# Three buffers instead of two for loaded weight pieces, with the low part written over the piece it is computed from

## What is computed

```python
def _layer(x, mem, cos, sin, w_in, ...):            # first block, twice
    h = x @ w_in
    ...
    y_mla, y_sb, y_fox, y_mem = ...
    merged = merged + merge_g[:, :, n] * (yb @ w_branch[n])
    out = merged @ w_out
    return _layer_norm(DEEPNORM_ALPHA * x + out, ln_g, ln_b)

def second_block(x, norm_g, w_in, w_out, ...):      # second block, twice
    h = _rmsnorm(x, norm_g[l])
    z = jnp.einsum('bsd,de->bse', h, w_in[l])
    ...
    q_a = _axial_rope(q_a, row, col)                # A; then B (window), D (differential), C (neighbourhood)
    k_a = _axial_rope(k_a, row, col)
    ...
    x = x + jnp.einsum('bsm,md->bsd', mix, w_out[l])
```

## Time and profile before

| | |
|---|---|
| median of 3 runs | 1443.2 us (1442.56 to 1445.12) |
| the profiled execution | 1443.2 us, its span 1441.4 us |
| TensorE matmul | busy 1371.9 us, 95% of the span |
| VectorE | busy 864.6 us, 60% |
| ScalarE | busy 732.6 us, 51% |
| GpSimd | busy 382.0 us, 27% |
| granted TensorE clock, mean | 0.988 of full speed |
| DMA | 94 GB/s on average over the span |

### The profile page before, as it was taken

One profiled execution on the slowest core, in us unless ns is written; L12 is line 12 of the kernel. 1 busy time (PEld: TensorE's weight loads), 2 busy tenths in 40 slices (PEclk: granted clock), 3 DMA queues, 4 the chain that ended last, 5 costly groups with the idle time before them and its releaser, 6 DMA issues.

```text
span 1441.4 us, 20050 instructions
## 1 busy us (share of the span) xinstructions
PE 1371.9 (95%) x7466; PEld 1064.1 (74%) x7466; DVE 864.6 (60%) x1513; ACT 732.6 (51%) x1561; POOL 382.0 (27%) x273
## 2 busy tenths in 40 slices
PE   7999999999989999999998899999899999999897
PEld 7877788778787777887776777776766877675665
DVE  4656536557662564455577675568656665578555
ACT  4555447655344554556554464446444554546443
POOL 2233131346131322213554111421012111421111
PEclk9999999999999999999999999999999999999999
DMA  7413551125353221112265532511323443511311
GB/s 236 118 31 92 115 142 48 52 72 224 102 161 65 55 88 59 59 48 66 77 229 167 130 74 59 125 59 52 103 67 90 111 93 70 113 59 23 118 51 59
DMA packets 185894, 135.65 MB, mean 94 GB/s; under 512 B 91334, under 2 KB 166726, under 8 KB 185798
## 3 DMA queue, kind: packets, MB, share of 16 engines
q1 hardware_dynamic: 182022, 120.22, 30.9%
q10 hardware_dynamic: 3776, 14.16, 2.5%
HBM read 122.03 MB, written 12.32 MB: 93 GB/s over the span
## 4 chain that ended last, share of the span: by engine, by line
PE 72%; DVE 14%; ACT 7%; issue 2%; POOL 2%; DMA 1%; SPq 1%; DVEq 0%; ACTq 0%; POOLq 0%
PE pb L1650 18%; PE pb L1652 17%; PE pb L1651 17%; PE pb L1741 5%; PE pb L1690 5%; PE pb L1717 5%; ACT prob L1797 3%; ACT tmp L1797 2%; DVE prob L2420 2%; DVE wl L2167 2%; SPq L2698 1%; PE pb L1772 1%; DMA tbias<-zscr 1%; PE pb L1726 1%; POOL wl L2564 1%
## 5 line engine op out<-in xcount | busy, mean ns | idle before, releaser
L2564 POOL TENSOR_TENSOR wl<-wr,wh 128x512 fp32r<-128x512 f32 x178 | 253.5, 1424 | 706.3 <-ACT wh L1817 702.1
L1650 PE MATMUL pb<-xh,wl 128*128 128x512 f32 (+1 forms) x880 | 350.2, 398 | 11.9 <-DVE wl L2167 6.4
L1652 PE MATMUL pb<-xh,wh 128*128 128x512 f32 (+1 forms) x880 | 324.8, 369 | 0.0
L1651 PE MATMUL pb<-xl,wh 128*128 128x512 f32 (+1 forms) x880 | 324.3, 369 | 0.0
L2167 DVE TENSOR_TENSOR wl<-wr,wh 128x512 fp32r<-128x512 f32 x208 | 167.2, 806 | 175.3 <-ACT wh L1817 175.1
L1817 ACT CAST wh<-wr 128x512 fp32r<-128x512 f32 (+1 forms) x386 | 220.1, 606 | 36.2 <-PE pb L1652 22.1
L1650 PEld LDWEIGHTS pb<-xh,wl 128*128 128x128 f32 x880 | 167.3, 190 | 65.6 <-issue 29.5
L1652 PEld LDWEIGHTS pb<-xh,wh 128*128 128x128 f32 x880 | 167.1, 190 | 29.1
L1651 PEld LDWEIGHTS pb<-xl,wh 128*128 128x128 f32 x880 | 167.9, 191 | 24.6 <-issue 4.3
L1797 ACT ACTIVATE tmp<-pb,cst 128x512 f32<-128x512 f32 (+3 forms) x128 | 83.0, 648 | 72.3 <-PE pb L1652 26.8
L1650 PE MATMUL pb<-wh,xl 128*128 128x256 f32 (+1 forms) x320 | 109.2, 341 | 10.9 <-DVE wl L2167 8.0
(11 more groups left out here) (198 smaller groups left out, 2339.0 us busy)
## 6 DMA issues: line engine op xcount, KB each, us to landing
wr<-w_in SPq DMA_DIRECT2D x39, 1024.0 KB, 5.3
wr<-w_out SPq DMA_DIRECT2D x14, 1024.0 KB, 5.1
wr<-w_in SPq DMA_DIRECT2D x48, 256.0 KB, 4.5
wr<-w_branch SPq DMA_DIRECT2D x48, 128.0 KB, 2.3
x<-prob SPq DMA_DIRECT2D x12, 512.0 KB, 3.6
wr<-w_mem_kv SPq DMA_DIRECT2D x4, 1024.0 KB, 5.8
prob<-x ACTq DMA_DIRECT2D x2, 2048.0 KB, 10.6
wr<-w_out SPq DMA_DIRECT2D x16, 256.0 KB, 4.2
```

The costliest lines, as they stand in the source:

```text
L1650: e.matmul(ps, ll, rh, start=start, stop=False)
L1651: e.matmul(ps, lh, rl, start=False, stop=False)
L1652: t = e.matmul(ps, lh, rh, start=False, stop=stop)
L2564: t = e.tensor_tensor(wl[:, j % 2, c0:c1], wr[:, j % 2, c0:c1], wh[:, j % 2, c0:c1].bitcast(F32), ALU.subtract)
```

## The change

`wl` gets three buffers, and the loaded pieces lie in the same memory: `wr` is allocated, given back, and `wl` takes its place, so that the low part is written over the loaded piece it is computed from. `wh` gets three buffers too. The memory is what it was, six times 8 KB a partition. The list of steps is unchanged; what changes is what three of them wait for:

- the load of piece j waits for the matmuls of piece j - 3 (before: for the casts and low parts of piece j - 2);
- the cast of piece j waits for the matmuls of piece j - 3 (before: j - 2);
- there are three landing semaphores `d_w` instead of two.

```diff
+N_LOADED, N_HIGH = 3, 3
...
-    wr = sb("wr", [P, 2, 2048])
-    wh, wl = sb("wh", [P, 2, 2048], F32R), sb("wl", [P, 2, 2048], F32R)
+    with nc.sbuf_tensor("wr", [P, N_LOADED, 2048], F32) as wr:
+        pass
+    wl, wh = sb("wl", [P, N_LOADED, 2048], F32R), sb("wh", [P, N_HIGH, 2048], F32R)
...
-                w.wait_ge(gemm, gemm.at(("w", j - 2)))
-                e.copy(wh[:, j % 2, c0:c1], wr[:, j % 2, c0:c1]).then_inc(w_hi.sem, w_hi.mark((j, c)))
+                w.wait_ge(gemm, gemm.at(("w", j - N_HIGH)))
+                e.copy(wh[:, j % N_HIGH, c0:c1], loaded(j, c0, c1)).then_inc(w_hi.sem, w_hi.mark((j, c)))
...
-                t = e.tensor_tensor(wl[:, j % 2, c0:c1], wr[:, j % 2, c0:c1], wh[:, j % 2, c0:c1].bitcast(F32), ALU.subtract)
+                hi = wh[:, j % N_HIGH, c0:c1].bitcast(F32)
+                t = e.tensor_tensor(wl[:, j % N_LOADED, c0:c1], loaded(j, c0, c1), hi, ALU.subtract)
...
-                if j >= 2:
-                    c = n_chunks(j - 2) - 1
-                    w.wait_ge(w_lo, w_lo.at((j - 2, c - c % 2)))
-                    w.wait_ge(w_lo2, w_lo2.at((j - 2, c - 1 + c % 2)))
-                    w.wait_ge(w_hi, w_hi.at((j - 2, c)))
-                v = wr[:, j % 2, 0:kc * n].rearrange("p (k c) -> p k c", k=kc)
+                w.wait_ge(gemm, gemm.at(("w", j - N_LOADED)))
+                v = loaded(j, 0, kc * n).rearrange("p (k c) -> p k c", k=kc)
```

More of the change, by code:

```diff
@@ L1482, in build @@
     d_x = [signal(f"d_x{i}", 16) for i in range(4)]
-    d_w = [signal(f"d_w{i}", 16) for i in range(2)]
+    d_w = [signal(f"d_w{i}", 16) for i in range(N_LOADED)]
     d_acc = [signal(f"d_acc{i}", 16) for i in range(4)]
@@ L1491, in weights, with loaded @@
         _, kc, n = WEIGHTS[j][0:3]
-        return (wl if lo else wh)[:, j % 2, 0:kc * n].rearrange("p (k c) -> p k c", k=kc)
-    def n_chunks(j):
-        return -(-WEIGHTS[j][1] * WEIGHTS[j][2] // 512)
+        part = wl[:, j % N_LOADED, 0:kc * n] if lo else wh[:, j % N_HIGH, 0:kc * n]
+        return part.rearrange("p (k c) -> p k c", k=kc)
+    def loaded(j, c0, c1):
+        return wr[:, j % N_LOADED, c0:c1]
     def pieces_of(j):
@@ L1812, in scalar_program @@
                 if j:
-                    w.wait_ge(d_w[j % 2], d_w[j % 2].at(j))
+                    w.wait_ge(d_w[j % N_LOADED], d_w[j % N_LOADED].at(j))
                 else:
                     w.wait_ge(d_first[c // 2], d_first[c // 2].at("w"))
-                w.wait_ge(gemm, gemm.at(("w", j - 2)))
-                e.copy(wh[:, j % 2, c0:c1], wr[:, j % 2, c0:c1]).then_inc(w_hi.sem, w_hi.mark((j, c)))
+                w.wait_ge(gemm, gemm.at(("w", j - N_HIGH)))
+                e.copy(wh[:, j % N_HIGH, c0:c1], loaded(j, c0, c1)).then_inc(w_hi.sem, w_hi.mark((j, c)))
             elif k == "feat":
@@ L2618, in sync_program @@
             elif k == "load":
-                j, g = s["j"], d_w[s["j"] % 2]
+                j, g = s["j"], d_w[s["j"] % N_LOADED]
                 name, kc, n = WEIGHTS[j][0:3]
-                if j >= 2:
-                    c = n_chunks(j - 2) - 1
-                    w.wait_ge(w_lo, w_lo.at((j - 2, c - c % 2)))
-                    w.wait_ge(w_lo2, w_lo2.at((j - 2, c - 1 + c % 2)))
-                    w.wait_ge(w_hi, w_hi.at((j - 2, c)))
-                v = wr[:, j % 2, 0:kc * n].rearrange("p (k c) -> p k c", k=kc)
+                w.wait_ge(gemm, gemm.at(("w", j - N_LOADED)))
+                v = loaded(j, 0, kc * n).rearrange("p (k c) -> p k c", k=kc)
                 for (k0, k1), (c0, c1), src, (p0, p1) in pieces_of(j):
```

## The result

| | before | after |
|---|---|---|
| median, same chip | 1443.6 us (4 runs) | 1470.3 us (4 runs, 1469.3 to 1471.9) |
| ratio to before | | 1.0175, 95% interval 1.0161 to 1.0188 |
| profiled execution: span | 1441.4 us | 1467.5 us |
| granted TensorE clock, mean | 0.988 | 0.985 |

The change makes the kernel slower: by 26.8 us between the two medians (1.85% of 1443.6) and by 26.1 us between the two profiled spans. The sign was right; the size was half.

The account below looks back on a forecast made before the run. TensorE bounds the kernel, busy 1371.9 of 1441.4 us, so edits count only where they open or close its holes. 7.0 + 3.5 + 4.0 - 1.5 = 13.0 us on 1443.2 gives 1456.2 us, range 1448 to 1462.

Parts of the forecast that it names:

- The sign: Whole kernel: slower, chance 0.89, against same 0.06 and faster 0.05.
- Tables, layer 1: A's tables behind Bg's load on SP, first layer: rotation 8.5 us late, loss 7.0 us, bounds 6.0 to 8.5.
- Then the logits of A: First layer, after the 6.0 us hole: TensorE waits 1.6 us more at A's logits, cut so both make 7.0.
- The bound 8.5: Upper end for A's tables, first layer: VectorE's whole 8.5 us delay reaches TensorE, nothing absorbed.
- Tables, layer 2: A's tables behind Bg's load, second layer: VectorE 4.9 us late, loss 3.5 us, bounds 2.4 to 4.9.
- Biases: Biases of C behind Dkv's load, both layers: 2.0 us each, 4.0 us together, bounds 0 and 5.0.
- The waits that go: Casts waiting for matmuls: 1.2 us gained at piece 33, 0.3 elsewhere, 1.5 us in all; bounds nothing and 2.92.
- For nearly all loads that is harmless: Loads going out later still land well ahead of their casts; tightest is piece 34, maybe 0.4 us.
- But what stands behind a load on SP has no such slack everywhere: SP's queue: A's tables and C's biases go out late behind loads, costing 7.0, 3.5 and 4.0 us.
- The gain of 28.5 us from earlier weights: First rival: earlier weights close TensorE's holes for low parts; up to 28.5 us gained, 1429.2 us; chance 0.05.
- The second rival: A's tables not late, only biases and the gain left: 1445.7 us, no change within 0.2%; chance 0.06.
- The third (late loads): Some four loads of short pieces (33 to 34, merge) late by up to 2 us each: 1464 us; chance 0.08.

Follow-up runs that it names:

- the kernel with the filled hole: Changed kernel plus 24 matmuls with unused result on TensorE just ahead of Akv's fifth row block, first layer; 1463.1 us, ratio 1.0137.

## Why the prediction was half right

**Tables, layer 1 (7.0; measured 8.5).** Right in mechanism and in the hole. The step that failed is "Then the logits of A": 1.0 us was put there for a second hole, and there was none. Instead the clock took 2.5. VectorE's catching up was taken at half a microsecond, by one operation that meets GpSimd; the kernel with the filled hole shows 2.4, since two long operations, of 1.67 and 1.83 us, shrink to 0.69 each. In the changed kernel itself VectorE even had to stand 1.0 us for TensorE at 860.63, so it had caught up before the last chunk. The bound 8.5, "nothing absorbed", was met by accident.

**Tables, layer 2 (3.5; measured 2.5).** A hole of 2.23 us, near the lower bound of 2.4, and no second one, by the same error.

**Biases (4.0; measured 7.1).** The holes grew from 1.24 and 0.97 to 3.36 and 2.77: 2.1 and 1.8 us, as forecast. Timelines of POOL and PE:

```profile
933.77 2.31 POOL L2606 TENSOR_TENSOR setB<-setB,cst 128x896 f32<-128x896 f32 x1 [11.68 <-DMA setB<-zscr]
...
944.37 0.50 PE L1654 MATMUL pb<-xh,wl 128*128 128x512 f32 x1 [3.36 <-POOL wl L2570]
...
1264.63 0.50 PE L1654 MATMUL pb<-xh,wl 128*128 128x512 f32 x1 [2.77 <-POOL wl L2570]
```

The other 3.2 us are the clock. The prediction had no term for it at any place: this is a failed step too, a cost put at nothing without a reason. The trace before had both the full clock (1.00) at the places where holes were to open and the lower one behind holes it already had (0.50 behind 2.37 us at 1099.64), and the two would have asked for a term. The Trainium skill (TensorE: Matmul & The Clock Gate, Why this matters for your kernels) says that long idle gaps between bursts of matmuls send the array's clock back to its half rate. The runs agree: 0.50 to 0.69 behind the four long holes, 1.00 behind the one of 6.0 us when it was filled. Counted from the rows, that is 2.5 + 1.6 + 1.6 = 5.7 us that the forecast lacked.

**The waits that go (-1.5; measured -1.4).** Right: 1.94 to 0.56 at the norm of piece 33, and the 22.1 us of casts standing for matmuls are gone from the list. What the forecast did not have is the hole of 0.61 us that opens 13 us later and takes 0.9 back. Timeline after:

```profile
414.79 1.09 PE L1616 MATMUL pb<-cst,prob 128*128 128x128 f32 x8 [0.56 <-DVE prob L2355]
```

Piece 34's cast stood 0.50 us for its load, as forecast (0.4).

**"For nearly all loads that is harmless" (0; measured 2.7 and 0.8).** This is the first of the two steps that failed outright. Landing times were taken from medians; load 29 took 9.4 us before, with ScalarE's transfers beside it, and 13.9 behind the first three of them. The Trainium skill (DMA: Bandwidth & Descriptors, Issuing engines are not separate DMA queues) says that what two engines issue shares the same 16 DMA engines and interleaves. The runs agree: 13.9 us behind x, the memory and a norm parameter (3.5 MB), 5.0 when they go out later.

**"But what stands behind a load on SP has no such slack everywhere" (0; measured 6.1).** This is the second, and the dearest. The sentence was right and the list under it was not complete: tables and biases only. The steps `spread` stand behind three loads, and the waits of VectorE showed 6.1 us for `zscr<-scr` before the change: already late, so any delay passes through. This one omission is 6.1 of the 13.1 us that were missing. The others: clock 5.7 less the second holes of about 2 that didn't come, piece 29 2.7, and 0.6 of small places and the start.

**Rivals.** The gain of 28.5 us from earlier weights did not come. With three high parts and SP's steps ahead, no cast waits for a matmul any more, and TensorE still stands 29.8 us for low parts: those holes did not hang on the casts' waits. The second rival (tables not late) fell; its remark that the loads landed ahead of their casts was not true of all, since three casts already stood 11.6 us for a load before. The third (late loads) was true in part, at two places instead of four.

## What to carry to other kernels

When a wait on an in-order queue is moved, list every step behind it, and look each up in the waits of the engine that reads it: one that is already waited for before the change passes every delay on. A third buffer is not yet an earlier transfer. What counts is when the release comes: three loaded pieces released by matmuls gave 1470.3 us, two released by their splitting 1443.6, four released by matmuls 1439.4, in the same memory. And price a new hole of TensorE by its length and by the clock behind it.

## What the hardware showed that I had not expected

- A hole of 6.0 us cost 2.5 to 2.6 us more at the lower clock level behind it; holes of 2.77 and 3.36 us cost 1.6; at one place in the program, the tables of the second layer, a hole of 2.23 us cost 0.3 more than its length in one kernel and one of 2.29 us cost 1.9 more in another.
- Time at the lower clock level moves between executions at places that no edit touches: the spreading cost 6.1 us in the changed kernel's profile and 8.0 in that of a kernel that first differs from it 600 us later.
- Issuing four DMAs took ScalarE 2.1 us at 338.9 and 3.7 us at 345.4, with the same four transfers.
